# Who makes the low parts of the second block's projection weights: GpSimd for all but one half, and part of a channel sum

## The reference

```python
h = rms_norm(x, g_mix)
z = einsum("bsd,de->bse", h, w_in) + b_in            # 1024 -> 7168
va, ga, xb, gb, sa, sb = split(z)                    # 1024, 1024, 1536, 1536, 1024, 1024
u = va * sigmoid(ga)
u = causal_depthwise_conv(u, conv_a_w, conv_a_b)     # 31 taps
u = silu(layer_norm(u, ln_g, ln_b))                  # mean and variance over 1024 channels
y_a = einsum("bsc,cd->bsd", u, w_a_out)
v = causal_depthwise_conv(xb, conv_b_w, conv_b_b)    # 4 taps
v = rg_lru(v, ...)                                   # gates, then a scan over time
y_b = einsum("bsc,cd->bsd", v * gelu(gb), w_b_out)
m = sigmoid(sa) * y_a + sigmoid(sb) * y_b
x = x + m @ w_o                                      # then an MLP, then a last norm
```

## Time and profile before

| what | us |
|---|---|
| median of 3 runs | 1048.51 (1048.03 to 1048.91) |
| the profiled execution's own time | 1048.01 |
| its span in the profile | 1046.3 |
| TensorE busy | 874.8 |
| VectorE busy | 522.4 |
| ScalarE busy | 350.2 |
| GpSimd busy | 122.9 |
| mean granted TensorE clock, share of full | 0.918 |

### The profile page before, as it was taken

One profiled execution on the slowest core, in us unless ns is written; L12 is line 12 of the kernel. 1 busy time (PEld: TensorE's weight loads), 2 busy tenths in 40 slices (PEclk: granted clock), 3 DMA queues, 4 the chain that ended last, 5 costly groups with the idle time before them and its releaser, 6 DMA issues.

```text
span 1046.3 us, 18002 instructions
## 1 busy us (share of the span) xinstructions
PE 874.8 (84%) x7849; PEld 703.9 (67%) x7849; DVE 522.4 (50%) x847; ACT 350.2 (33%) x471; POOL 122.9 (12%) x61
## 2 busy tenths in 40 slices
PE   8999989775747646485648999999999999999997
PEld 8998856342424223242324799599999999988985
DVE  4567643230211203130212699999997766544542
ACT  5755111000100000000002654577657455523521
POOL 1052000000000000000010688407010000000000
PEclk9999998986877878787879999999999999999999
DMA  9827799999999999999999556144487544465421
GB/s 340 265 86 317 324 377 428 423 427 426 428 428 429 427 430 429 428 428 428 430 427 391 162 171 199 43 161 163 158 264 245 212 165 162 162 209 193 162 80 41
DMA packets 86624, 299.99 MB, mean 287 GB/s; under 512 B 12265, under 2 KB 50597, under 8 KB 74149
## 3 DMA queue, kind: packets, MB, share of 16 engines
q1 hardware_dynamic: 86421, 299.13, 72.8%
q10 hardware_dynamic: 144, 0.00, 0.0%
HBM read 298.07 MB, written 1.05 MB: 286 GB/s over the span
## 4 chain that ended last, share of the span: by engine, by line
PE 53%; DMA 32%; DVE 10%; ACT 2%; issue 2%; SPq 1%; POOL 0%; DVEq 0%; ACTq 0%
DMA mem<-in_w_up 25%; PE PS L1905 12%; PE PS L1906 12%; PE PS L1907 12%; PE PS L2126 8%; DVE PS L1658 5%; DMA mem<-in_w_down 3%; PE PS L2139 3%; DMA mem<-in_w_in 2%; DMA mem<-in_w 2%; DVE ring_rest L1633 1%; PE PS L2112 1%; ACT mlp_hi L1104 1%; PE PS L1879 1%; PE PS L2152 1%
## 5 line engine op out<-in xcount | busy, mean ns | idle before, releaser
L2126 PE MATMUL PS<-mem 128*32 128x256 f32 x2048 | 157.5, 474 | 137.0 <-DMA mem<-in_w_up 136.5
L2126 PEld LDWEIGHTS PS<-mem 128*32 128x32 f32 x2048 | 82.1, 136 | 214.0 <-issue 145.5
L1907 PE MATMUL PS<-HT_hi,ring_rest 128*128 128x256 f32 x752 | 212.6, 283 | 0.0
L1907 PEld LDWEIGHTS PS<-HT_hi,ring_rest 128*128 128x128 f32 x752 | 143.6, 191 | 0.0
L1433 DVE TENSOR_TENSOR mem<-mem,PS 128x128 f32<-128x128 f32 x32 | 12.1, 379 | 262.2 <-ACT mem L882 262.2
L1905 PE MATMUL PS<-HT_hi,z_hi 128*128 128x256 f32 x432 | 122.7, 284 | 0.3 <-POOL ring_rest L698 0.3
L1906 PE MATMUL PS<-HT_rest,z_hi 128*128 128x256 f32 x432 | 122.2, 283 | 0.0
L882 ACT ACTIVATE mem<-PS 128x128 f32<-128x128 f32 x32 | 8.9, 277 | 273.4 <-PE PS L2126 273.4
L1796 DVE TENSOR_TENSOR ring_rest<-mem,mlp_hi 128x4096 fp32r<-128x4096 f32 x16 | 70.8, 4424 | 57.8 <-ACT mlp_hi L1104 57.6
L698 POOL TENSOR_TENSOR ring_rest<-mem,z_hi 128x2048 fp32r<-128x2048 f32 x19 | 87.5, 4620 | 88.3 <-DVE mem L1708 46.8
L1658 DVE SCALAR_TENSOR_TENSOR PS<-mem,CAW,PS 128x256 f32<-128x256 f32 x232 | 91.3, 481 | 0.0
(11 more groups left out here) (352 smaller groups left out, 1765.7 us busy)
## 6 DMA issues: line engine op xcount, KB each, us to landing
mem<-in_w_gate SPq DMA_DIRECT2D x32, 2048.0 KB, 16.6
mem<-in_w_up SPq DMA_DIRECT2D x32, 2048.0 KB, 21.0
mem<-in_w_down SPq DMA_DIRECT2D x31, 2048.0 KB, 12.8
mem<-in_w SPq DMA_DIRECT2D x16, 2048.0 KB, 8.5
mem<-in_w_in SPq DMA_DIRECT2D x30, 1024.0 KB, 5.3
mem<-in_w_in SPq DMA_DIRECT2D x4, 2048.0 KB, 18.4
mem<-in_w_b_out SPq DMA_DIRECT2D x4, 1536.0 KB, 8.8
mem<-in_w_out SPq DMA_DIRECT2D x4, 1024.0 KB, 12.0
```

What stands on the lines that cost most here:

```text
L1907: ins = nc.tensor.matmul(dst, s_rest, m_hi, start=False, stop=stop and n == len(terms) - 1, skip_group_check=True)
L2126: ins = nc.tensor.matmul(PS[SLOTS * j:SLOTS * (j + 1), bank, 0:2 * F_STRIP].rearrange("p (w n) -> p w n", w=2), xg[:, k, :], w[:, :, k, F_ ...
```

## The change

`REST_LRU` and `REST_SCAN` go, with VectorE's seven low parts and GpSimd's two waits. GpSimd makes the low parts of halves 2 to 27 one after the other. After half 20 it adds, chunk pair by chunk pair, chunks 0 to 1 and 2 to 3 of `CU` into two chunks (`two_sums`, where the gate table of the recurrence lay), and after half 21 chunks 4 to 5. VectorE no longer reduces over eight chunks: it adds the last pair, and then the two sums. The counts of `sum_ready` move by one.

```diff
-REST_LRU, REST_SCAN = (16, 17, 18), (23, 24, 25, 26)
+CHANNEL_SUMS = (20, 21)
...
+        two_sums = Z[:, Z_GA:Z_GA + 2, :]
...
             for n in range(2, IN2_HALVES):
-                if n == REST_LRU[0]:
-                    pool.wait_ge(lru_square, RG)
-                if n == REST_SCAN[0]:
-                    pool.wait_ge(h_ready, RG)
-                if n not in REST_LRU + REST_SCAN:
-                    if n - 1 in REST_LRU + REST_SCAN:
-                        pool.wait_ge(z_rest_ready, n)
-                    rest_half(n)
+                rest_half(n)
+                if n == CHANNEL_SUMS[0]:
+                    pool.wait_ge(lru_ps, RG)
+                    for i in range(2):
+                        pool.wait_ge(tap_step[i], TAPS_A * 3)
+                    link(nc.gpsimd.tensor_tensor(two_sums, CU[:, 0:2, :], CU[:, 2:4, :], ALU.add))
+                if n == CHANNEL_SUMS[1]:
+                    nc.gpsimd.tensor_tensor(two_sums, two_sums, CU[:, 4:6, :], ALU.add).then_inc(sum_ready, 1)
...
-            rest_half(REST_LRU[0])
...
-                if g < 2:
-                    rest_half(REST_LRU[1 + g])
...
-                rest_half(REST_SCAN[g])
...
-            nc.vector.tensor_reduce(Z[:, Z_GA, :], CU.rearrange("p k t -> p t k"), AX_X, ALU.add).then_inc(sum_ready, 1)
+            dve.wait_ge(sum_ready, 2)
+            link(nc.vector.tensor_tensor(two_sums, two_sums, CU[:, 6:8, :], ALU.add))
+            nc.vector.tensor_tensor(two_sums[:, 0, :], two_sums[:, 0, :], two_sums[:, 1, :], ALU.add).then_inc(sum_ready, 1)
...
-            pe.wait_ge(sum_ready, 2)
+            pe.wait_ge(sum_ready, 3)
...
-                    pe.wait_ge(sum_ready, 3)
+                    pe.wait_ge(sum_ready, 4)
```

## The result

The changed kernel takes 1066.2 us (median of 4 runs, 1062.75 to 1069.72) against 1048.4 for the kernel before in the same comparison: a ratio of 1.0173, 95% interval 1.0152 to 1.0194. It is 17.8 us slower; 20.7 were forecast. Its four runs lie in two pairs, at 1062.8 and at 1069.7, that is 14.4 and 21.3 us above the kernel before, and the median falls between them, where no run is. Lines moved by a few: L707 before is L708, L698 is L699, L1702, 1707 and 1708 kept their numbers, L1719 to 1726 became L1717 to 1724.

What follows compares the result with a forecast made beforehand. TensorE was busy 84% of the span, with h_ready reaching four having 0.4 us of slack. Delay 19.0 plus clock 1.7 gave 20.7 us on 1048.0, so 1068.7, median 1069.2; range 1057 to 1077.

Steps and rivals of the forecast that it cites:

- h has no slack: Before half 26: the fourth h_ready has 0.4 us of slack, so delaying it costs nearly the delay's whole length.
- the walk: Estimated timeline from 696.3 us, engines alternating whole instructions: fourth h at 776.5, next projection at 791.7, 19.0 us later.
- the holes: TensorE's idle spots before half 19 (0.33 us) and the next projection (1.27 us); removing them could win 1.6 us.
- Turns of whole instructions: VectorE's two-SBUF-input and GpSimd's SBUF-reading instructions exclude each other whole, 4.55 us per 2048 columns; chance 0.60.
- shorter holds: GpSimd yields between pieces of a long instruction: +15 us with the clock, 1063.5; chance 0.22 together with a mixture.
- The first stretch: VectorE's twelve two-input instructions after pair 2's convolution end at 736.9 us instead of 713.9.
- several turns in a row for VectorE: Sign against the forecast: GpSimd's low parts then come late and TensorE waits for L698 directly.
- The scans: Four scan groups, 15.3 us, with one turn of 4.55 for half 26; fourth h ready at 776.5 instead of 755.8.
- Stalls of TensorE: Some 4 us at half 21 and again at 22, covered by the later one of about 12 us before half 26.
- The clock: TensorE's granted clock drops after the hole before half 26, costing 1.7 us.
- The sum: Next projection 19.0 us later plus 1.7 for the clock: 20.7 us on the profiled execution's 1048.0.
- No hindrance: Squares, multiply-adds and scans keep out of GpSimd's way; only the holes' 1.6 us are won, 1046.9; chance 0.10.

Runs made afterwards that it cites:

- the lower level: The changed kernel, unchanged, executed twice more with a profile each: 1062.8 and 1062.7 us, with the first stretch ending at 730.6 in the first.
- 45 extra matmuls: The changed kernel plus 45 extra matmuls into a free bank before TensorE's half 26: 1064.95 us, ratio 1.0168.
- the run without reads: The changed kernel, but from half 16 GpSimd's low parts become memsets that read nothing; its two sums still read: 1046.05 us, ratio 0.9990 to the kernel before.

## Why the prediction was right

- *h has no slack*: right. In the four profiles of the changed kernel the next projection follows the fourth h: h is ready at 777.0 and it begins at 795.0, 18.0 us behind; on the lower level 770.9 and 788.6, 17.8 behind; in the other two 17.0 and 16.9. Where the clock did not fall (45 extra matmuls) it is 15.4, and the walk had 15.2. Before it was 755.8 and 772.7, 16.9 behind, without the clock's term and with the holes and the slack in it.
- *Turns of whole instructions*, 4.55 us for 2048 columns: right, shown by the lengths above and by the run without reads. The first rival, shorter holds, falls: VectorE's 0.95 became 5.3, a whole low part more but for what had already run when it asked. (That rival's own sum is a little short: eleven turns of 2.3 us are 25.3, not 24.)
- *The first stretch*: 736.9 forecast, 736.3 measured in the profiled run (735.3 and 736.6 in the two other upper profiles), but not by the walk's own order. I had GpSimd's half 17 slip in behind the first product. In the profiled run it was issued at 698.9 and waited for the last two products (6.2 us long); in a lower run it was issued at 696.3, during the first product, and three more products and the square went ahead of it (8.4 us long). These are several turns in a row for VectorE, which the prediction had named as a sign against itself; it stayed at these few instructions, and TensorE never waited for L699 directly. The agreement to 0.6 us is partly luck: the products began 0.8 us later than the walk's 696.3, so the stretch itself was 1.4 us shorter than in the walk.
- *The scans*: one turn forecast and one measured (6.23 us for three scans where 1.85 were), with another 1.0 us on the product ahead of them, which waited for the end of half 25; h at 776.5 forecast, 777.0 measured. On the lower level it was 770.9 and 771.4.
- *Stalls of TensorE*: 12.3 us before half 26 forecast, 11.8 measured. The two of some 4 us at halves 21 and 22 were one of 5.5, and there was one of 1.3 near 702 that I had not foreseen; all are covered by the last one, as forecast.
- *The clock*: 1.7 us forecast, 2.5 measured in the profiled run and 1.4, 1.5 and 2.3 in the three others, so the size was right on the whole. It was borrowed from a stand of 2 us; behind 12 us the clock was at half for 5.6 us in the profiled run and for 3.3 to 5.3 in the others, and what makes these differ was not tried.
- *The sum*: 20.7 forecast, 21.7 for the profiled run, 17.8 for the median. The step that fell short is the count of turns: it is not fixed. In about half of the runs it is one less, which the walk could not tell, because it took the exponential's time from one execution; a load of the weights 1.3 us earlier or later goes with it.
- *No hindrance*: wrong for this kernel, right as a sum, since the run without reads went as that rival said to within 0.6 us.

## What to carry to other kernels

A wait that keeps GpSimd idle may be there to keep its reads away from VectorE's, not for the data. Before work is moved to GpSimd, list the VectorE instructions with two SBUF inputs that will run beside it: each may cost one whole instruction of GpSimd, and short ones on the path pay most (0.95 us became 5.3). If the two must run together, put GpSimd's reads beside VectorE's work on PSUM, as the pauses did. Where one link has no slack, relieving an engine that is 99% busy wins little: 18.8 us off VectorE were worth about 1 us where nothing was hindered (the run without reads), and three adds for one reduction brought about as much, if anything.

## What the runs showed that I had not expected

- VectorE can keep GpSimd out for several turns: GpSimd's half 17 took 8.4 us in a lower run while the rest of one product, three more and a square ran at their usual 0.95. Three scans in a row let it in (14.93 us instead of 1.85, three turns). Neither the products nor the three scans wait for VectorE's own results in between, so what makes the difference is not known.
- A load that lands 1.3 us later goes with an end about 6 us later, by way of one more turn on VectorE; this is read from the four profiles of the changed kernel and was not tried.
- Three dependent adds of 1024, 512 and 256 columns take 2.4 us where one reduction over the same 2048 takes 3.87.
